# The step sizes of a Mamba-2 mixer: the series behind the reciprocal moved from VectorE to GpSimd

## The reference

```python
z, xbc, dt_raw = jnp.split(u @ w_in, [D_INNER, D_INNER + CONV_DIM], axis=-1)
...
dt = jax.nn.softplus(dt_raw.astype(F32) + dt_bias.astype(F32))   # (B, T, 32 heads)
a = -jnp.exp(a_log.astype(F32))
y, h_last = ssd_scan(xs, dt, a, bm, cm, ssm0)
```

## Time and profile before

| | |
|---|---|
| Time, median of 3 runs | 1203.46 us (1202.77 to 1203.70) |
| Profiled execution: its own time | 1201.87 us |
| Its span in the trace | 1200.1 us, 26585 instructions |
| TensorE busy | 1189.0 us (99%), 9800 products |
| VectorE busy | 875.0 us (73%), 1398 instructions |
| ScalarE busy | 689.9 us (57%), 1118 instructions |
| GpSimd busy | 246.1 us (21%), 351 instructions |
| Conversions L1515 | 367, mean 1253 ns |
| HBM | 200 GB/s over the span |

### The profile page before, as it was taken

One profiled execution on the slowest core, in us unless ns is written; L12 is line 12 of the kernel. 1 busy time (PEld: TensorE's weight loads), 2 busy tenths in 40 slices (PEclk: granted clock), 3 DMA queues, 4 the chain that ended last, 5 costly groups with the idle time before them and its releaser, 6 DMA issues.

```text
span 1200.1 us, 26585 instructions
## 1 busy us (share of the span) xinstructions
PE 1189.0 (99%) x9800; PEld 1159.0 (97%) x9800; DVE 875.0 (73%) x1398; ACT 689.9 (57%) x1118; POOL 246.1 (21%) x351
## 2 busy tenths in 40 slices
PE   8999999999999999999999999999999999999998
PEld 8999999998988899999999999999998899999998
DVE  7767646999999868677745987788468767667448
ACT  7445435776686657555545865555368765444345
POOL 1000002422222101222344323232026410000001
PEclk9999999999999999999999999999999999999999
DMA  8765554754445365867787577656742256555552
GB/s 284 246 210 185 181 175 142 255 188 168 162 163 165 131 210 177 321 223 255 264 303 244 200 272 271 232 167 235 252 159 80 83 171 213 175 178 189 176 178 87
DMA packets 62144, 239.08 MB, mean 199 GB/s; under 512 B 7288, under 2 KB 8480, under 8 KB 57696
## 3 DMA queue, kind: packets, MB, share of 16 engines
q1 hardware_dynamic: 55728, 197.01, 48.8%
q0 software_dynamic: 6064, 40.66, 9.3%
q10 hardware_dynamic: 288, 0.54, 0.1%
HBM read 226.87 MB, written 13.39 MB: 200 GB/s over the span
## 4 chain that ended last, share of the span: by engine, by line
PE 93%; DVE 4%; ACT 1%; issue 1%; DMA 0%; POOL 0%; SPq 0%; ACTq 0%; DVEq 0%
PE bank L477 29%; PE bank L478 29%; PE bank L479 28%; DVE wlo L1515 1%; PE bank L842 1%; PE bank L837 1%; PE bank L863 1%; DVE xl L1534 1%; ACT under L1430 1%; DMA raw<-weights 0%; PE bank L893 0%; ACT whi L1048 0%; PE bank L811 0%; PE bank L823 0%; PE bank L824 0%
## 5 line engine op out<-in xcount | busy, mean ns | idle before, releaser
L1515 DVE TENSOR_TENSOR wlo<-raw,whi 128x1024 fp32r<-128x1024 f32 x367 | 458.5, 1253 | 236.8 <-ACT whi L1048 235.4
L477 PE MATMUL bank<-xh,whi 128*128 128x264 f32 x2008 | 576.6, 287 | 4.1 <-DVE wlo L1717 2.4
L478 PE MATMUL bank<-xl,whi 128*128 128x264 f32 x2008 | 570.0, 284 | 0.0
L479 PE MATMUL bank<-xh,wlo 128*128 128x264 f32 x2008 | 569.6, 284 | 0.0
L1048 ACT ACTIVATE whi<-raw 128x1024 fp32r<-128x1024 f32 x367 | 385.4, 1054 | 250.6 <-PE bank L479 237.2
L477 PEld LDWEIGHTS bank<-xh,whi 128*128 128x128 f32 x2008 | 379.0, 189 | 8.3 <-issue 4.7
L478 PEld LDWEIGHTS bank<-xl,whi 128*128 128x128 f32 x2008 | 379.2, 189 | 0.8
L479 PEld LDWEIGHTS bank<-xh,wlo 128*128 128x128 f32 x2008 | 377.4, 188 | 0.0
L477 PE MATMUL bank<-hh,whi 128*128 (+1 forms) x896 | 255.6, 285 | 0.3 <-ACT gu L1398 0.3
L479 PE MATMUL bank<-hh,wlo 128*128 (+1 forms) x896 | 255.1, 285 | 0.0
L478 PE MATMUL bank<-hl,whi 128*128 (+1 forms) x896 | 254.4, 284 | 0.0
(11 more groups left out here) (331 smaller groups left out, 1018.3 us busy)
## 6 DMA issues: line engine op xcount, KB each, us to landing
raw<-weights SPq DMA_DIRECT2D x367, 512.0 KB, 3.6
under<-ssm POOLq DMA_DIRECT2D x8, 1024.0 KB, 6.2
xact<-ssm POOLq DMA_DIRECT2D x8, 1024.0 KB, 7.4
out_ssm_s<-xact POOLq DMA_DIRECT2D x8, 1024.0 KB, 5.4
xact<-dtx_rows POOLq DMA_DIRECT2D x5, 1024.0 KB, 10.3
zs<-dtx_rows POOLq DMA_DIRECT2D x2, 1024.0 KB, 14.5
x<-xT SPq DMA_DIRECT2D x4, 264.0 KB, 5.6
xact<-stat_rows POOLq DMA_DIRECT2D x2, 528.0 KB, 6.4
```

What stands on the lines that cost most here:

```text
L477: pe.matmul(out, whi[:, w, c], rh, start=start, stop=False)
L478: pe.matmul(out, whi[:, w, c], rl, start=False, stop=False)
L479: return pe.matmul(out, wlo[:, w, c], rh, start=False, stop=stop)
L1515: dve.tensor_tensor(wlo[:, s, :], raw[:, s, :], whi[:, s, :].bitcast(F32), ALU.subtract).then_inc(lo_ready, 1)
```

## The change

VectorE keeps the first two of the fifteen steps (2 + e and the reciprocal), and in slot 1 it does them ahead of that slot's conversion instead of behind it. The rest runs on GpSimd between its histories and its constants, after a wait for VectorE's two steps. Where VectorE did a multiply and an add in one instruction, GpSimd does two, so the 13 steps become 22, and `DT_STEPS` goes from 15 to 24. The semaphore, the tiles and the waits of ScalarE are the same ones.

```diff
-DT_STEPS = 15
+DT_STEPS = 24
+DT_DVE = 2
...
-            t_, e_, m_, r_, q_, s2_, a_ = (xact[:, 8 + k, 0:66] for k in range(7))
+            t_, e_, r_ = xact[:, 8, 0:66], xact[:, 9, 0:66], xact[:, 11, 0:66]
             n_dt = [0]
...
-            def dt_series(ks):
-
-                for k in ks:
-                    dt_step(dve.scalar_tensor_tensor(out=a_, in0=a_, scalar=1.0 / k, in1=s2_, op0=ALU.add, op1=ALU.mult))
-
             def dt_start():
 
                 dve.wait_ge(dt_a_step, 4)
                 dt_step(dve.tensor_scalar(r_, e_, 2.0, None, ALU.add))
                 dt_step(dve.reciprocal(r_, r_))
-                dt_step(dve.tensor_tensor(q_, e_, r_, ALU.mult))
-                dt_step(dve.tensor_tensor(s2_, q_, q_, ALU.mult))
-                dt_step(dve.tensor_scalar(a_, s2_, 1.0 / 17, None, ALU.mult))
-
-            def dt_end():
-
-                dt_step(dve.scalar_tensor_tensor(out=a_, in0=a_, scalar=1.0, in1=q_, op0=ALU.add, op1=ALU.mult))
-                dt_step(dve.scalar_tensor_tensor(out=a_, in0=a_, scalar=2.0, in1=m_, op0=ALU.mult, op1=ALU.add))
-                dt_step(dve.tensor_scalar(t_, a_, avec[:, :], -1.0, ALU.mult, ALU.mult))
-                assert n_dt[0] == DT_STEPS
+                assert n_dt[0] == DT_DVE
...
                 if kind == "z":
                     z_take(s_, i)
+                if s_ == 1:
+                    dt_start()
                 if s_ - 2 in DEC_AT:
                     decode_read(DEC_AT.index(s_ - 2))
...
                 if 0 < s_ < len(SIN) and not chunks:
                     ahead("sin", 0, s_)
-                if s_ == 1:
-                    dt_start()
-                if s_ == 2:
-                    dt_series((15, 13, 11, 9))
-                if s_ == 3:
-                    dt_series((7, 5, 3))
-                    dt_end()
...
             ins.then_inc(hist_ready, 1)
             pool.wait_ge(hist_ready, 1)
 
+            t_, e_, m_, r_, q_, s2_, a_ = (xact[:, 8 + k, 0:66] for k in range(7))
+            n_dt = [DT_DVE]
+
+            def dt_step(ins):
+                link(pool, dt_d_step, n_dt, ins)
+
+            pool.wait_ge(dt_d_step, DT_DVE)
+            dt_step(pool.tensor_tensor(q_, e_, r_, ALU.mult))
+            dt_step(pool.tensor_tensor(s2_, q_, q_, ALU.mult))
+            dt_step(pool.tensor_scalar(a_, s2_, 1.0 / 17, None, ALU.mult))
+            for k in (15, 13, 11, 9, 7, 5, 3):
+                dt_step(pool.tensor_scalar(a_, a_, 1.0 / k, None, ALU.add))
+                dt_step(pool.tensor_tensor(a_, a_, s2_, ALU.mult))
+            dt_step(pool.tensor_scalar(a_, a_, 1.0, None, ALU.add))
+            dt_step(pool.tensor_tensor(a_, a_, q_, ALU.mult))
+            dt_step(pool.tensor_scalar(a_, a_, 2.0, None, ALU.mult))
+            dt_step(pool.tensor_tensor(a_, a_, m_, ALU.add))
+            dt_step(pool.tensor_scalar(t_, a_, avec[:, :], -1.0, ALU.mult, ALU.mult))
+            assert n_dt[0] == DT_STEPS
+
             pool.tensor_copy(ident_r, ident)
```

## The result

The changed kernel takes 1207.29 us (median of 6 runs, 1206.80 to 1209.61) against 1203.12 for the kernel before in the same runs (6, 1202.41 to 1203.90): the ratio is 1.0044, 95% interval 1.0034 to 1.0054. It is slower: by 4.2 us in the medians, by 5.3 us in the ratio, with 4.1 to 6.5 by the interval. The profiled execution has a span of 1205.6 us against 1200.1.

A forecast was written before the change was run, and what follows sets the result against it. TensorE bounds the kernel, with only a 1.5 us stand at unit 9 to win. The late series (+2.84) and colliding constants (+0.7) sum to +3.5 us: 1205.4 profiled, 1207.0 as median with 1.6 added, range 1204.0 to 1209.6.

The forecast's parts named there:

- the path behind it: From the late series through ScalarE's gathers and VectorE's taps to unit 9, which was to start 2.84 us late.
- Removing the thirteen steps: On VectorE: 3.7 us less work, by itself enough to win all of TensorE's 1.5 us at unit 9.
- the order: VectorE's two steps ahead of slot 1's conversion: its later end hidden by TensorE, 1.2 us cover, otherwise 0.9 us cost.
- The series on GpSimd: 22 linked steps on GpSimd: 8.0 us alone, but held by VectorE's conversions, so ending at 227.0 instead of 223.53.
- the price of a step with one immediate operation: In GpSimd's series at 66 columns: 0.33 us a step, ten such steps.
- seven steps by: During VectorE's conversions of slots 1 to 4: two GpSimd steps a round, seven done at 221.45.
- the casts beside the taps: GpSimd's constants, run beside VectorE's taps and the conversion for unit 9, were to cost 0.7 us.
- Two short stands should leave it: TensorE's clock was to stay at 1.00 (2.4 GHz) despite stands of about 2.6 and 1.7 us.
- the sign of 1 to 2.5 us there: The new trace was to show TensorE standing 1 to 2.5 us at unit 9.
- GpSimd keeps up: Rival: GpSimd steps slip by the conversions, series ends at 223.2, time 1202.5 us; chance 0.10.
- Dear steps: Rival: GpSimd series steps cost 0.6 us each, the last 15 take 9.0 us, +7.0 us, 1210.5; chance 0.12.
- the wait is covered: Rival: TensorE or ScalarE has more work ready, so the late series costs within 1 us, 1204; chance 0.08.

The follow-up runs named there:

- e2: Changed kernel with the 22 GpSimd series steps replaced by 22 linked memsets of the same tiles, which only write; 1200.90 us.
- e6: Kernel before with four terms of the series (17, 15, 13, 11) left out, series still on VectorE; 1201.62 us.
- e10: Kernel before with two terms of the series (1/17 and 1/15) left out on VectorE; 1201.46 us.
- e1: Kernel before with only the order changed: VectorE's first steps ahead of slot 1's conversion, all fifteen steps on VectorE; 1202.63 us.
- e8: Changed kernel with three of the seven immediate adds given a second operation, a multiply by 1.0; 1207.59 us (one run).
- e3: Changed kernel with GpSimd's constants moved from behind the series to its slot 8; 1208.45 us.
- e5: Changed kernel with four more terms of the series, 8 linked GpSimd steps more; 1210.38 us.
- e4: Changed kernel with four terms of the series left out, 8 linked GpSimd steps fewer; 1205.04 us.
- e7: Changed kernel with both ScalarE gathers moved from slot 4 to slot 6, behind that slot's rounding; 1208.86 us.
- e9: Changed kernel with the leanest GpSimd series: four terms fewer, two-operation immediate steps, 13 linked steps in place of 22; 1202.64 us.

## Why the prediction was right

The forecast was 1207.0, and 1207.29 was measured, with the mechanism that was forecast: a late series, behind it the gather, the taps and the take of unit 7. That the two agree to 0.3 us is luck. In the stage the trace has +5.0 us where the forecast had +3.5, and 3.5 lies below the interval of 4.1 to 6.5; the forecast put its +3.5 on a base of 1203.46, the kernel before took 1203.12 in the six runs, and the medians are only 4.2 us apart. By terms, the gather came 1.8 us later than forecast and the path behind it was 0.3 us shorter: 3.5 + 1.8 - 0.3 = 5.0.

**All of it hangs on the series' end.** Shown: with 8 steps less the gather starts 3.54 us sooner and the sums 3.53; with 8 more the gather starts 3.22 us later and the sums 3.54. Between the two kernels the gather is 5.10 us later and unit 9 5.02. ScalarE's gather waits on GpSimd, and VectorE's taps on ScalarE, as forecast (VectorE was to be idle from 221.7; it is from 221.88 - 0.64 = 221.2 on the time scale of before).

**VectorE's part.** Removing the thirteen steps was to give all of TensorE's 1.5 us; e2 shows that it would (no stand at all) if the result came in time, and e6 and e10 show the price of a step, 0.26 us. The first step alone took 0.19 us instead of 0.66, and the order cost nothing (e1).

**The series on GpSimd: the term that was mis-sized.** On the time scale of before it was to have its last but one step done at 226.5 and was done at 229.00 - 0.64 = 228.4, 1.8 us later. Two causes, +1.1 and +1.3 us, with 0.6 against them because the fourth step ended sooner than the forecast's seventh (221.48 - 0.64 = 220.8 against 221.45). First the price of a step with one immediate operation, 0.33 us by the forecast from a two-operation row, 0.47 in fact; e8 shows it is the form (0.13 us for each of the three steps where it was tried; the series has ten). A step of two tensors was 0.42 instead of 0.38. The one with a per-partition scalar (0.34) was cheaper than the 0.5 taken. Together the 15 steps that the forecast left for the free stretch take 15 x 0.44 = 6.6 us, not 5.5. Second, the forecast let seven steps by during the four conversions, one waiting and one in each gap; four got by, and the three others took 3 x 0.44 = 1.3 us of the free stretch. In the gap the next step comes at 217.06, the conversion at 217.05: it lost by a hundredth. In e3 and e5, where one conversion began 0.03 to 0.05 us behind the step and not ahead of it, the fourth step slipped in (0.41 us) and the series was 0.3 us shorter. That a step in a conversion waits for its end was right each time.

**The path behind it.** From the gather to unit 9 the forecast had 234.27 - 226.6 + 0.7 = 8.4 us and 8.1 was measured; the casts beside the taps cost 0.3 us of it instead of 0.7 (e3).

**TensorE's clock.** "Two short stands should leave it" failed: the stand at the transposes was 4.5 us, not 2.6, and the clock fell. The row it rested on has TensorE idle for 0.45 of 4 us, which says nothing of a stand of 2.6. In the changed kernel the low clock costs nothing, since unit 9 waits 0.5 us for VectorE all the same; it filled what would have been a stand of about 2 us (e4, whose clock stayed at 1.00 and whose gather stands as far ahead of unit 9, has 2.0). In e3, e5 and e7 TensorE at the low clock is the late one. So the stand at unit 9 was 0.5 us and not 1.7, and the sign of 1 to 2.5 us there failed.

**The rivals.** That GpSimd keeps up fell with the first four steps. Dear steps were half true: 0.44 us each, not 0.6. That the wait is covered fell with the 4.5 us at the transposes.

Not tried: the series with the constants ahead of it on GpSimd, and how long a stand lets the clock fall; both stay open.

## What to carry to other kernels

A chain of small dependent steps is worth the engine that ends it soonest, not the engine with the most idle time: VectorE spent 3.7 us on the steps and GpSimd took 13.7 (215.74 to 229.41), and three engines stood behind the result. Before moving work to GpSimd, lay its timeline beside VectorE's two-input instructions, for while VectorE is at one GpSimd gets through one reading step at most. Cheapest of all is to do fewer steps where they are: two terms below the rounding gave 0.5 us by the trace (e10), where the leanest series on GpSimd, with four terms fewer, gave nothing (e9).

## What the runs showed of the hardware that I had not expected

- An immediate step with one operation takes 0.38 to 0.39 us on GpSimd at 128 x 66, with two operations 0.25 to 0.26 (e8, e9).
- Linked GpSimd steps that only write (128 x 66) take 0.21 us each also while VectorE converts (e2).
- GpSimd holds VectorE as well as the reverse, and time saved in one place was lost again in full in another: conversions of 1.67 and 1.64 us behind casts of 0.61 (e1).
- TensorE's granted clock was 0.50 behind stands of 4.5, 4.2, 4.1, 6.4 and 7.7 us (after, e3, e8, e7, e5) and stayed 1.00 with stands of 0.9 and 2.0 us (e4). At 0.50 the products start 0.22 us apart instead of 0.12, and the low clock held for 3.5 us behind the transposes in the changed kernel and for 5.6 and 6.2 in e3 and e5.
